# Two transformer blocks in split fp32: which engine makes the low parts of the weights in three projections

## What is computed

```
x = x + (g_nsa * o_nsa + g_conv * o_conv + g_mem * o_mem) @ w_out
x = x + 0.5 * swiglu_ffn(rmsnorm(x, ffn2_norm_g), ffn2_w_in, ffn2_w_out)
...
h = h + merge_heads(mix) @ sb_w_o[i]          # and fox_w_o[j] in the second layer
h = h + swiglu(rms_norm(h, ffn_norm_g[i]), ffn_w_gu[i], ffn_w_d[i])
```

## Time and profile before

| what | value |
|---|---|
| median of 3 runs | 2808.38 us (2806.64 to 2808.88) |
| the profiled execution | 2807.5 us, of it 2805.7 us in the span of the trace |
| TensorE busy | 2752.2 us, 98% |
| DVE busy | 1586.1 us, 57% |
| ACT busy | 1399.2 us, 50% |
| POOL busy | 1133.8 us, 40%, of it 753.4 us in `rest` (L3243, 290 instructions) |
| mean granted clock of TensorE | 0.996 |

### The profile page before, as it was taken

How to read it: one execution, slowest core, us unless ns; L and a number is a source line. 1 busy time by engine, 2 the same in 40 slices (tenths; PEclk the granted TensorE clock), 3 DMA queues, 4 the chain that set the end, 5 groups by cost and what they waited for, 6 DMA issues and landing times.

```text
span 2805.7 us, 40994 instructions
## 1 busy us (share of the span) xinstructions
PE 2752.2 (98%) x15824; PEld 2344.6 (84%) x15824; DVE 1586.1 (57%) x2858; ACT 1399.2 (50%) x2480; POOL 1133.8 (40%) x637
## 2 busy tenths in 40 slices
PE   8999999999999999999999998999999999899999
PEld 6888888777778887999788877999887777899887
DVE  5333354655554367777444548777437666777733
ACT  4322234555654546556235556556245565655523
POOL 3444443322235334554433224554443334455443
PEclk9999999999999999999999999999999999999999
DMA  4443242222223222333221112333322342233322
GB/s 156 156 139 131 91 153 76 74 87 79 78 84 115 86 78 93 107 105 107 88 81 61 58 41 94 106 106 112 101 87 86 114 128 94 87 106 106 115 85 83
DMA packets 92906, 276.02 MB, mean 98 GB/s; under 512 B 15239, under 2 KB 21639, under 8 KB 92072
## 3 DMA queue, kind: packets, MB, share of 16 engines
q1 hardware_dynamic: 82796, 257.10, 27.7%
q0 software_dynamic: 9440, 15.16, 1.5%
q10 hardware_dynamic: 476, 1.12, 0.1%
HBM read 271.13 MB, written 10.58 MB: 100 GB/s over the span
## 4 chain that ended last, share of the span: by engine, by line
PE 88%; DVE 6%; ACT 3%; issue 2%; DMA 1%; POOL 1%; SPq 0%; DVEq 0%; ACTq 0%; POOLq 0%
PE bank L624 10%; PE bank L626 10%; PE bank L625 10%; PE bank L957 7%; PE bank L961 7%; PE bank L959 7%; PE bank L695 7%; PE bank L697 7%; PE bank L696 7%; PE bank L1253 1%; PE bank L984 1%; PE bank L1025 1%; PE bank L1011 1%; DVE h_lo L2469 1%; PE bank L1394 1%
## 5 line engine op out<-in xcount | busy, mean ns | idle before, releaser
L3243 POOL TENSOR_TENSOR w_lo<-raw,w_hi 128x1024 fp32r<-128x1024 f32 (+1 forms) x290 | 753.4, 2603 | 1209.5 <-ACT w_hi L1546 1209.5
L1546 ACT ACTIVATE w_hi<-raw 128x1024 fp32r<-128x1024 f32 (+1 forms) x292 | 327.9, 1129 | 690.7 <-PE bank L626 535.3
L3256 POOL TENSOR_TENSOR lo_s<-raw_s,hi_s 128x512 fp32r<-128x512 f32 x198 | 259.9, 1314 | 292.8 <-ACT hi_s L1607 236.5
L957 PE MATMUL bank<-a_hi,w_hi 128*128 128x512 f32 x808 | 323.4, 400 | 4.6 <-DVE a_lo L2590 3.8
L961 PE MATMUL bank<-a_lo,w_hi 128*128 128x512 f32 x808 | 318.8, 395 | 0.0
L959 PE MATMUL bank<-a_hi,w_lo 128*128 128x512 f32 x808 | 317.5, 393 | 0.0
L624 PE MATMUL bank<-h_hi,w_hi 128*128 128x512 f32 x704 | 275.2, 391 | 6.7 <-POOL w_lo L3243 2.5
L625 PE MATMUL bank<-h_hi,w_lo 128*128 128x512 f32 x704 | 274.7, 390 | 0.0
L626 PE MATMUL bank<-h_lo,w_hi 128*128 128x512 f32 x704 | 274.5, 390 | 0.0
L695 PE MATMUL bank<-b_hi,hi_s 128*128 128x256 f32 x792 | 226.0, 285 | 16.2 <-DVE b_lo L2490 10.2
L624 PE MATMUL bank<-a_hi,w_hi 128*128 128x512 f32 x600 | 234.4, 391 | 0.0
(11 more groups left out here) (423 smaller groups left out, 6284.3 us busy)
## 6 DMA issues: line engine op xcount, KB each, us to landing
raw<-in_w SPq DMA_DIRECT2D x228, 512.0 KB, 3.3
raw<-in_w SPq DMA_DIRECT2D x64, 704.0 KB, 4.0
u_raw<-in_ws SPq DMA_DIRECT2D x66, 512.0 KB, 3.7
raw_s<-in_ws SPq DMA_DIRECT2D x132, 256.0 KB, 3.2
bias_rows<-bias_table POOLq DMA_DIRECT2D x4, 2048.0 KB, 29.5
strip<-bias_rows SPq DMA_DIRECT2D x16, 448.0 KB, 4.1
cw<-in_cw POOLq DMA_DIRECT2D x4, 1024.0 KB, 6.2
terms<-forget_cumsum SPq DMA_DIRECT2D x8, 512.0 KB, 8.4
```

What stands on the lines that cost most here:

```text
L957: mm(dst, high[:, w], hi[:, b], start=b == 0, stop=False)
L1546: act(w_hi[HI[v]][:, 0:nk * P], raw[LO[v]][:, 0:nk * P], ACT.Copy).then_inc(sem("w_hi_ready"), 1)
L3243: eng.tensor_tensor(w_lo[LO[v]][:, 0:nk * P], raw[LO[v]][:, 0:nk * P], w_hi[HI[v]][:, 0:nk * P].bitcast(F32), ALU.subtract).then_inc(sem(" ...
L3256: eng.tensor_tensor(lo_s[i][:, :], src, hi_s[i][:, :].bitcast(F32), ALU.subtract).then_inc(sem(done), 1)
```

## The change

Where POOL made the low parts of all eight units of `wo0`, `sb_o` and `fox_o`, it now makes those of the first three of each and goes on to its `pairs`. DVE makes those of the other five: at the end of its steps k = 0 to 4 it subtracts for unit k + 3. Before the first of them it waits until POOL has finished unit 2, so that the counter stays in order. In all, 15 subtractions of 128x1024 change the engine. No transfer and no wait of another engine is changed.

```
@@ VectorE @@
+            def weight_low(v):
+
+                nk = BLOCKS[v]
+                wait("w_hi_ready", v + 1)
+                eng.tensor_tensor(w_lo[LO[v]][:, 0:nk * P], raw[LO[v]][:, 0:nk * P],
+                                  w_hi[HI[v]][:, 0:nk * P].bitcast(F32), ALU.subtract).then_inc(sem("w_lo_ready"), 1)
@@ VectorE, pairs, end of step k @@
+                    if k == 0:
+                        wait("w_lo_ready", U0[name] + 3)
+                    if k < NCH - 3:
+                        weight_low(U0[name] + k + 3)
@@ GpSimd @@
-            rests(U0["qmem"] + 3, U0["ffn1_out"])
+            rests(U0["qmem"] + 3, U0["wo0"] + 3)
             pairs(1)
-            rests(U0["ffn1_out"], U0["ffn2_out"])
+            rests(U0["ffn1_out"], U0["sb_o"] + 3)
             pairs(2)
...
-            rests(U0["fox_kv"] + 19, U0["ffn3_out"])
+            rests(U0["fox_kv"] + 19, U0["fox_o"] + 3)
             pairs(3)
```

## The result

The changed kernel takes 2817.43 us (median of 6 runs, 2814.56 to 2819.41) against 2808.63 us for the kernel before beside it: a ratio of 1.0031, with a 95% interval of 1.0020 to 1.0042. It is slower by about 8.8 us. The forecast was 2813.9 us in a range of 2809.5 to 2818.5, with 0.45 on slower by more than 0.2% and 0.50 on no change. The range held the time, the direction was that of the sum, and the size was 5.5 us where 8.8 were measured. A second set of 6 runs gave 1.0033 (1.0021 to 1.0045). That the range held was partly luck: the median of the second set, 2818.78 us, lies just above it.

What follows compares the result with a forecast made beforehand. The prediction took DVE's steps in the three projections as the bound: +5.70 - 3.76 - 0.1 = +1.84 us a stage, +5.5 us for three, so 2813.9 us against the median of 2808.4; range 2809.5 to 2818.5.

Steps and rivals of the forecast that it cites:

- What bounds: In the three projections DVE's eight steps set the end; 1 us more there makes the kernel 1 us longer.
- What it adds: Five subtractions at the end of DVE's steps 0 to 4, 1.14 us each: 5.70 us a stage, none in gaps.
- What it removes: POOL's five `w_lo` a stage stop holding up DVE's L2489 and L2495: 3.76 us a stage saved.
- What moves: POOL's `a11(0)` runs earlier, freeing L2490 (1.11 us) but stretching a step 1 `z` (1.0): 0.1 us a stage gained.
- TensorE's side: TensorE stalls 1.9 us before unit 4; its later waits for `b1_lo` and L2502 cover this, costing little more than nothing.
- Rival (3): TensorE becomes the bound: stalls before units 4 and 7 and a lower clock, 2817 to 2821 us; chance 0.10.
- (1): `a11(0)` lands between DVE instructions reading PSUM, port cost nearly goes: +0.84 a stage, 2810.9 us; 0.20 together with (4).
- (2): Freed POOL also gets its three other parts off DVE's step 7 `z`: -1.4 a stage, 2804.3 us; chance 0.05.
- (4): DVE isn't alone the bound; the 5.70 partly vanish in waits for ACT: 2811.1 us; 0.20 together with (1).

Runs made afterwards that it cites:

- the kernel with the low parts left out: The changed kernel without its 15 subtractions, TensorE reading the high part instead, so the low parts of units 3 to 7 are missing; 2797.72 us, ratio 0.9967.
- the filled waits: The changed kernel plus 12 and 16 unread matmuls in TensorE's waits for `b1_lo` and `b2_lo` behind the units; 2813.98 us, ratio 1.0024.
- the same matmuls in the kernel before: The kernel before plus 12 and 16 unread matmuls in TensorE's two waits behind the units; 2807.20 us, ratio 0.9998.

## Why the prediction came out as it did

**What bounds: right.** DVE's eight steps set the end. Over the whole table the time follows them: from 33.3 to 49.3 us a stage it goes from 2797.7 to 2844.6, that is 46.8 us for 3 x 16.0 = 48.0. Between these ends the kernels leave a line of 3 us for each 1 us of a stage's steps by up to 2 us: drawn from the kernel with the low parts left out, the kernel before lies 2.0 us under it and the changed kernel 2.2 above, so their difference of 8.8 us is about half steps and half something else.

**What it adds: right, and 0.3 us a stage too much.** The sum had 5.70 us a stage for the five, and they cost 5.4. None stood in a gap; the same instruction moved into the gap nearly vanished.

**What it removes: right.** L2489 and L2495 came down to their undisturbed 0.42 and 0.49 us. With the place of `a11(0)` the rows gave 3.76 + 0.1; the kernel without the subtractions showed 3.8.

**What moves: right.** `a11(0)` landed on `z` at 1064.5, for 1.39 - 0.485 = 0.90 us where I had 1.0. By the Trainium skill, page "SBUF — State Buffer", section "Who interferes with whom", the port pair that the two engines share is an exclusive lock; the estimate worked out from it was a whole L3256, 1.3 us. Measured is 0.4 us less: POOL's operation began 0.35 us ahead of the `z` that it held up, while the `z` before that one was still running, unharmed.

The steps together: forecast +1.84 a stage, measured +1.6.

**TensorE's side: the step that failed.** "At worst the new stall brings that on in unit 4 instead; it then takes up the two waits, and costs little more than nothing." I had priced the lower clock only as something that the stall ahead of unit 4 could bring, and had left the second wait at its 1.2 us, where 2.7 were measured. The fall in the units did occur (in stage 3 of the profile, 2374 to 2378, and in stages 2 and 3 of the second one) and was covered, as said. What I didn't follow was the first wait: that its fall kept the second wait short, and that with a shorter first wait this fall could come behind the second one instead. In the sum this term stood at nothing. In the first profile what stands beside the steps is 2.5 + 0 + 1.6 us behind the stages, less the 1.7 that came back, and 0.6 elsewhere; by the profile with the filled waits, 1.1 of the 2.5 is the fall behind the second wait and 1.4 the one behind the third. Filling the first two waits took 2.0 to 2.5 us off the ratio's time with the change and nothing without it. The falls behind the third wait are read from the profiles; no run here removes them.

The forecast of 5.5 us consists of 4.8 that were there and 0.7 too much on DVE, and lacks 3 to 4 us beside the steps, of which the filled waits show 2.0 to 2.5 to be the clock's. Rival (3) named a lower clock and up to 7 us for it, but put it in the units, where it was harmless. Rivals (1), (2) and (4) are out: the `z` was hit, the `z` of step 7 were held up as before (1.39 and 1.48 us at 1097 and 1098), and the 5.4 us came in full.

What stays open: which of a kernel's waits is followed by a fall isn't settled by these profiles. The wait of 1.8 us at 1339 was followed by one before and not after, with the same length.

## What to carry to other kernels

When an engine that is busy in a chain takes over work from one that has time, weigh the place of each instruction and not the engines' totals: here one 128x1024 subtraction cost 1.14 us, 0.2 us or nothing, by whether it stood on DVE's chain, in a long enough wait of DVE for ScalarE, or on POOL beside instructions that read PSUM. Where two waits of TensorE follow each other, don't take the second for free cover: look in which of them the clock falls, and what work comes behind it. And if the expected effect is a few microseconds in 2800, read more than one execution: the profile here was 2 us faster than the median of its own kernel.

## What the hardware showed that I had not expected

One kernel, the changed one, has executions in two groups whose middles are 4.4 us apart, with mean granted clocks of 0.994 and 0.996 to 0.997. With the waits filled, 11 executions lie within 1.8 us (2812.98 to 2814.74), all at 0.997. The clock isn't all that varies, though: with the same matmuls in the kernel before, ten executions at 0.998 go from 2805.54 to 2809.63 us, and an eleventh, at 1.000, takes 2802.70.

POOL gets its turn between two DVE instructions that read SBUF: `a11(0)` was released when `s3(0)` ended and started at 1064.51, a `z` was running from 1064.34 and ended undisturbed in 0.48 us, and the next `z` was held to 1.39.

Three subtractions of 128x240 on DVE took 3.39 us beside POOL's `w_lo` of 2.40 us, and 1.28 us with POOL idle: of POOL's 2.40 us, 2.1 came on top of their own time.
